# Rows for the experts turned once, the norm's weights applied at the first gathered tile, and a router product in four column groups

## The chip, the cores and the metric

The kernel runs on one core of a Trainium2 chip. The metric is device time in microseconds (us). The engines go by these names: PE multiplies matrices (PEld is its weight load), ACT and DVE evict and split tiles, POOL does small arithmetic and issues indirect transfers, SP issues the loads of the weight stream. Engines run on their own and meet at semaphores.

## What is computed

One inference step of a decoder with two layers, on 288 token rows (256 prompt, 32 sample) of 1024 features. Each layer mixes tokens and then applies a feed-forward part; in the second layer that part is a choice of 2 out of 8 experts:

```python
h = rmsnorm(x, g_ffn[1])
logits = h @ w_router                    # 8 per row
vals, idx = top_k(logits, 2); wts = softmax(vals)
for e in range(8):
    out += gates[:, e] * (silu(h @ wg[e]) * (h @ wu[e])) @ wd[e]
x = x + out
```

where `rmsnorm(x, g)` is `x * rsqrt(mean(x*x) + eps) * g`: one factor for each row (the code's `rstd`) and one for each feature (the norm's weights `g`).

## The kernel before

All weights come from HBM once, as a stream of chunks of 128 x 2048 fp32 (1 MB) into a ring of six buffers `raw`. ACT copies a chunk into a rounded high part `whi` (L311), DVE subtracts for the low part `wlo` (L315), and PE forms each product from three matmuls (L327 to L329). Rings of three `whi` and `wlo` let PE hold ACT back, and ACT DVE.

`xT` holds the rows turned, features on the 128 partitions in eight blocks `k`. The stretch between the last product of layer 1's mixing and the first product of expert 0 is what the change touches. It goes like this, each engine in its own written order:

- ACT makes `xg[k] = xT[k] * g` (`with_gain`, L580; g lies there one to a partition) and squares, POOL adds the squares up in `ssum` (L448).
- PE forms the router product (`route`, L1805): eight matmuls, one for each `k`, into 8 partitions of one bank, then the sums of squares (`sums_of_x`, L1536). DVE copies the logits (L1210) and the means (L949), and POOL makes `rstd` from them (L452).
- PE turns `xg` back into rows, six blocks of four transposes each (`row_block`, L1858), the first of them ahead of the turned logits (L1866).
- DVE takes the logits (L1215), finds the two largest and the mask, signals `pos_in`, clears the third row tile of `xm` (L1230, signal `xm_blank`), and after PE's counts (L1875, L1877) makes the place of each row: `rounds_ok`, the selection matrix `sel` (L1250), `to_row` (L1261). Then it splits a chunk (L315).
- ACT evicts the six blocks into `xm`, times `rstd` (L761). PE turns `xT` itself into rows, six more blocks, which ACT evicts into `x` (L766), to which the experts' results are added.
- PE gathers the rows of expert 0 (`gather`, L1897): `xm` times `sel` gives eight blocks of 128 features x 128 places in two banks. ACT rounds each bank into `gT_hi` (`gathered_hi`, L792), DVE subtracts for `gT_lo` (`gathered_lo`, L1340), and PE begins expert 0 with chunks 66 and 67, then 68.
- POOL scatters the rows of `xm` to HBM, six indirect transfers (L515, signal `x_spread`), from which ACT's queue loads the rows of expert 1 onwards (L833). ACT waits there, in its own order, ahead of all that follows in expert 0.

The rounding copies in expert 0's first steps need a table load on ACT (before L792), as do SiLU and Exp later (L797, L878).

Of the kernel before, what the change touches and what calls it, by code (L numbers as in the profile page):

```python
# [64 lines left out]
FILL_LEFT = NE * SLOTS - FILL * (UP_CH - UP_CH % RAWS)  # L65
SETTLES = 12
NEVER = -3.0e38
NORMS = 7
# [24 lines left out]
def build(nc, io):  # L93
# [3 lines left out]
    with ctx:  # L97
# [19 lines left out]
        def phase():  # L117
            return ExitStack()

        early = phase()  # L120
        ph = lambda n, s, d=F: early.enter_context(nc.sbuf_tensor(n, s, d))
# [50 lines left out]
        with phase() as room:  # L172
# [18 lines left out]
            xm = ph("xm", [P, 3, D])  # L191
            logitsT = ph("logitsT", [NE, NT])
            logits = ph("logits", [P, 3, NE])
# [50 lines left out]
        for width in (W_POOL, W_SP, W_SPS, G_V, S_POOL):  # L244
# [31 lines left out]
            "y_hi_out", "y_out", "y_last_out", "y_half_done", "scat_done", "x_added", "fin_out",  # L276
            "to_row_out", "from_row_out", "got_added", "zero_set", "crossed_in", "sP_out", "hx_packed", "pair_in", "pair_out", "left_hi", "left_lo", "xn_blank", "xg_out", "xm_blank", "xm_turned", "ticked", "settled")}
        zero_filled, x_spread, rows_in, y_saved = (sem(n) for n in ("zero_filled", "x_spread", "rows_in", "y_saved"))
# [14 lines left out]
        GOT_STEPS = {4: (0, 1), 5: (2,), 6: (3, 4), 7: (5,), 8: (6, 7), 9: (8,), 10: (9, 10), 11: (11,)}  # L293
        TURN_BANKS = (0, 1, 6)
        ROW_BANKS = (3, 4, 5, 6, 7, 2)
# [75 lines left out]
        def _(sp):  # L371
# [26 lines left out]
            for c in range(C_MIX1, C_MOE):  # L398
                load_chunk(sp, (c, c), c % RAWS)
            sp.wait_ge(S["dT_done"], 4 * DEPTH)  # L400
            for c in range(C_MOE, C_MOE + RAWS):
                load_chunk(sp, (c, c), c % RAWS)
            sp.wait_ge(S["rounds_ok"], 1)
            n_rounds = nc.sync.value_load(rounds[0:1, 0:1], min_val=1, max_val=MAX_ROUNDS)
            with nc.sync.Fori(0, n_rounds) as r:
                done = nc.sync.snap(1 >> r)
                with nc.sync.Fori(done, ROUND_CH // RAWS) as i:
                    for j in range(RAWS):
                        row = C_MOE + RAWS * i + j
                        load_chunk(sp, (row + ROUND_CH * r, row), (C_MOE + j) % RAWS)  # L410
            sp.dma_start(g_rows, io["g_final"]).then_inc(gain_in, 16)
            for t in range(3):
# [8 lines left out]
        def _(pool):  # L421
# [44 lines left out]
            pool.wait_ge(chunk_used, DEPTH * KV_CH)  # L466
            zero_pair(qs[0:1])
            for l in range(DEPTH):
                if l:
# [31 lines left out]
                if l == 0:  # L501
# [5 lines left out]
                    fill(pool, y_slots[Y_ROWS:Y_ROWS + P, :], P)  # L507

            pool.wait_ge(zero_filled, 16 * FILLS)
            pool.wait_ge(S["xm_out"], 6)  # L510
# [31 lines left out]
        def _(act):  # L542
# [212 lines left out]
            act.wait_ge(rstd_ok, rstd_event(1, E_FFN))  # L755
            for t in range(3):
                if t == 2:
                    act.wait_ge(S["xm_blank"], 1)
                for n in range(2):
                    act.wait_ge(S["xm_turned"], 2 * t + n + 1)  # L760
                    nc.scalar.activation(xm[0:ROWS[t], t, n * 512:(n + 1) * 512], bank[ROW_BANKS[2 * t + n]][0:ROWS[t], :],  # L761
                                         ACT.Copy, scale=rstd[0:ROWS[t], N_FFN, t:t + 1]).then_inc(S["xm_out"], 1)
            for t in range(3):
                for n in range(2):
                    act.wait_ge(S["rows_turned"], 2 * t + n + 1)
                    nc.scalar.activation(x[0:ROWS[t], t, n * 512:(n + 1) * 512], bank[ROW_BANKS[2 * t + n]][0:ROWS[t], :],  # L766
                                         ACT.Copy).then_inc(S["x_rows_out"], 1)

# [3 lines left out]
            with nc.scalar.Fori(0, n_rounds) as r:  # L772
# [17 lines left out]
                def gathered_hi(q, j, b):  # L790
                    act.wait_ge(S["gat_done"], 2 * q + b + 1)
                    nc.scalar.activation(gT_hi[:, j, 4 * b:4 * b + 4, :].rearrange("p a b -> p (a b)"), bank[b][:, :],  # L792
                                         ACT.Copy).then_inc(S["gat_hi"], 1)

                def silu_of(cb, s, extra=0):
# [68 lines left out]
                for b in range(2):  # L864
                    gathered_hi(q, 0, b)
                for slot in range(3):
# [29 lines left out]
        def _(dve):  # L896
# [312 lines left out]
            dve.wait_ge(S["logit_done"], 1)  # L1209
            V.tensor_copy(logitsT[:, :], bank[2][0:NE, 0:NT]).then_inc(S["logitT_out"], 1)  # L1210
            mean_of_x(2, N_FFN, 1)
# [60 lines left out]
            with V.Fori(0, n_rounds) as r:  # L1272
# [65 lines left out]
                def gathered_lo(q, j, b):  # L1338
                    dve.wait_ge(S["gat_hi"], 2 * q + b + 1)
                    V.tensor_tensor(gT_lo[:, j, 4 * b:4 * b + 4, :].rearrange("p a b -> p (a b)"), bank[b][:, :],  # L1340
                                    gT_hi[:, j, 4 * b:4 * b + 4, :].rearrange("p a b -> p (a b)").bitcast(F), ALU.subtract)\
                        .then_inc(S["gat_lo"], 1)

                def keep_selT():
                    dve.wait_ge(S["selT_done"], r + 1)
                    V.tensor_copy(selT[:, :], bank[0][:, 0:NT]).then_inc(S["selT_out"], 1)
# [108 lines left out]
                for b in range(2):  # L1455
                    gathered_lo(q, 0, b)
                with V.Fori(V.snap((1 >> r) * 2), 3) as m:
# [29 lines left out]

            dve.wait_ge(gain_in, 16)
            for t in range(3):
# [7 lines left out]
        def _(pe):  # L1497
# [95 lines left out]
            for l in range(DEPTH):  # L1593
# [208 lines left out]
                def route(k):  # L1802

                    pe.wait_ge(S["xg_out"], k + 1)
# [56 lines left out]
            pe.wait_ge(S["xg_out"], 4)  # L1861
            row_block(0, 0, xg).then_inc(S["xm_turned"], 1)
            pe.wait_ge(S["logitT_out"], 1)
            pe.wait_ge(ms_out, 3)
            for t in range(3):
                last = T.transpose(bank[1][0:ROWS[t], L_AT + t * NE:L_AT + (t + 1) * NE], logitsT[:, t * P:t * P + ROWS[t]],  # L1866
                                   ident[0:NE, 0:NE])
            last.then_inc(S["logit_turned"], 1)
            pe.wait_ge(S["xg_out"], KD)
            for t, n in ((0, 1), (1, 0), (1, 1), (2, 0), (2, 1)):  # L1870
                row_block(t, n, xg).then_inc(S["xm_turned"], 1)

# [6 lines left out]
            last.then_inc(S["pos_done"], 1)  # L1879
            for t in range(3):  # L1880
                for n in range(2):
                    pe.wait_ge(S["xm_out"], 2 * t + n + 1)
                    row_block(t, n, xT).then_inc(S["rows_turned"], 1)
# [308 lines left out]
```

## Time and profile before

| | us |
|---|---|
| median of three runs | 1460.87 (1460.55 to 1461.44) |
| span of the profiled execution | 1460.6 |
| PE busy | 1432.0 (98%) |
| DVE busy | 1178.8 (81%) |
| ACT busy | 958.8 (66%) |
| POOL busy | 113.0 (8%) |
| load of weights, 427.91 MB on SP's queue | 77.0% of 16 engines' span |

The span of the profile, from the first to the last instruction, is 0.2 us below the median of the runs. Busy time of pipelined matmuls overlaps, so how full PE is has to be read from the chain of waits: the work that ended last, followed back step by step to what released it.

### The profile page before, as it was taken

To read this page: it belongs to the slowest core of one execution; us is meant where nothing else is said; L and a number is where in the kernel's file an instruction comes from. 1 tells how busy PE (TensorE), PEld (TensorE's weight loads), DVE (VectorE), ACT (ScalarE), POOL (GpSimd) and SP (SyncE) were. 2 spreads that over 40 slices of the span, in tenths; PEclk is the share of its full clock that TensorE was granted. 3 is DMA by queue.
4 is the path that set the end of the run, shared out by engine and by line. 5 is a ranking of instruction groups with operands and counts; after the bars stand their busy time and mean duration, and the time that the engine had idled before them with its cause. 6 is when DMAs were issued, how large, how long until landed. Compare 5 with 4: busy or idle time off the path is not lost.

```text
span 1460.6 us, 21408 instructions
## 1 busy us (share of the span) xinstructions
PE 1432.0 (98%) x7550; PEld 1218.0 (83%) x7550; DVE 1178.8 (81%) x1125; ACT 958.8 (66%) x929; POOL 113.0 (8%) x125
## 2 busy tenths in 40 slices
PE   7999999999999999999999999999999999999997
PEld 5999999999988788888888888888888887888785
DVE  5767766645675888988988888898898888899997
ACT  7646343344566877777777777777777777777774
POOL 1312111001313000000000000000000000002100
PEclk9999999999999999999999999999999999999999
DMA  9643687655433999999999999999999999999992
GB/s 358 259 151 142 235 277 260 227 190 184 179 117 117 385 367 363 367 381 371 349 398 365 356 396 367 357 376 362 373 349 407 366 356 390 365 361 364 402 397 109
DMA packets 67425, 456.31 MB, mean 312 GB/s; under 512 B 7652, under 2 KB 7946, under 8 KB 15911
## 3 DMA queue, kind: packets, MB, share of 16 engines
q1 hardware_dynamic: 59687, 427.91, 77.0%
q0 software_dynamic: 5680, 20.49, 3.6%
q10 hardware_dynamic: 2016, 7.34, 1.2%
q8 instruction: 27, 0.44, 0.1%
q14 instruction: 15, 0.12, 0.0%
HBM read 434.10 MB, written 21.88 MB: 312 GB/s over the span
## 4 chain that ended last, share of the span: by engine, by line
PE 89%; DVE 4%; ACT 4%; DMA 1%; issue 1%; POOL 0%; DVEq 0%; SPq 0%; ACTq 0%
PE bank L328 28%; PE bank L327 27%; PE bank L329 27%; DVE wlo L315 2%; PE bank L1926 2%; ACT whi L311 1%; DMA raw<-in_stream 1%; ACT junk L553 1%; PE bank L1686 0%; DMA stage<-in_mem 0%; PE bank L1904 0%; PE bank L1555 0%; PE bank L1554 0%; DVE stage L1112 0%; PE bank L1858 0%
## 5 line engine op out<-in xcount | busy, mean ns | idle before, releaser
L315 DVE TENSOR_TENSOR wlo<-raw,whi 128x2048 fp32r<-128x2048 f32 x400 | 916.1, 2293 | 153.6 <-ACT whi L311 152.4
L311 ACT ACTIVATE whi<-raw 128x2048 fp32r<-128x2048 f32 x400 | 765.3, 1915 | 157.0 <-PE bank L329 148.7
L327 PE MATMUL bank<-whi,gT_hi 128*128 128x512 f32 x896 | 362.8, 405 | 0.0
L328 PE MATMUL bank<-wlo,gT_hi 128*128 128x512 f32 x896 | 354.8, 396 | 0.0
L329 PE MATMUL bank<-whi,gT_lo 128*128 128x512 f32 x896 | 354.3, 395 | 0.0
L329 PEld LDWEIGHTS bank<-whi,gT_lo 128*128 128x128 f32 x896 | 168.2, 188 | 39.8
L327 PEld LDWEIGHTS bank<-whi,gT_hi 128*128 128x128 f32 x896 | 168.4, 188 | 36.2
L328 PEld LDWEIGHTS bank<-wlo,gT_hi 128*128 128x128 f32 x896 | 168.7, 188 | 35.7
L328 PE MATMUL bank<-wlo,eT_hi 128*128 128x512 f32 x448 | 177.4, 396 | 0.0
L327 PE MATMUL bank<-whi,eT_hi 128*128 128x512 f32 x448 | 176.5, 394 | 0.9 <-DVE eT_lo L1355 0.9
L329 PE MATMUL bank<-whi,eT_lo 128*128 128x512 f32 x448 | 177.2, 395 | 0.0
L327 PE MATMUL bank<-hT_hi,whi 128*128 128x288 f32 x512 | 153.1, 299 | 1.9 <-DVE hT_lo L917 1.6
L328 PE MATMUL bank<-hT_lo,whi 128*128 128x288 f32 x512 | 152.1, 297 | 0.0
L329 PE MATMUL bank<-hT_hi,wlo 128*128 128x288 f32 x512 | 152.0, 297 | 0.0
L801 ACT ACTIVATE eT_hi<-bank 128x256 fp32r<-128x256 f32 x112 | 43.2, 386 | 118.0 <-PE bank L1926 118.0
L327 PEld LDWEIGHTS bank<-whi,eT_hi 128*128 128x128 f32 x448 | 84.1, 188 | 22.3 <-DVE wlo L315 1.3
L328 PEld LDWEIGHTS bank<-wlo,eT_hi 128*128 128x128 f32 x448 | 84.1, 188 | 20.5
L329 PEld LDWEIGHTS bank<-whi,eT_lo 128*128 128x128 f32 x448 | 84.1, 188 | 19.9
L327 PEld LDWEIGHTS bank<-hT_hi,whi 128*128 128x128 f32 x512 | 96.7, 189 | 2.7 <-DVE hT_lo L917 2.1
L328 PEld LDWEIGHTS bank<-hT_lo,whi 128*128 128x128 f32 x512 | 96.5, 189 | 0.1
L329 PEld LDWEIGHTS bank<-hT_hi,wlo 128*128 128x128 f32 x512 | 96.6, 189 | 0.0
L528 POOL TENSOR_TENSOR tick<-half 128x3 f32<-128x3 f32 x2 | 2.6, 1288 | 863.3 <-DMA y_slots<-y_rows 863.3
(268 smaller groups left out, 1410.5 us busy)
## 6 DMA issues: line engine op xcount, KB each, us to landing
raw<-in_stream SPq DMA_DIRECT2D x401, 1024.0 KB, 5.3
x_slots<-zero POOLq DMA_DIRECT2D x18, 640.0 KB, 5.7
rows_e<-x_slots ACTq DMA_DIRECT2D x7, 512.0 KB, 6.5
y_slots<-y_rows ACTq DMA_DIRECT2D x7, 512.0 KB, 6.3
const<-in_const SPq DMA_DIRECT2D x1, 1192.0 KB, 22.3
raw<-in_stream SPq DMA_DIRECT2D x2, 512.0 KB, 6.9
stage<-in_mem SPq DMA_DIRECT2D x2, 512.0 KB, 7.2
xn<-in_x_prompt SPq DMA_DIRECT2D x1, 1024.0 KB, 10.4
```

The costliest lines, as they stand in the source:

```text
L311: nc.scalar.activation(whi[:, slot % SPL, :], raw[:, slot, :], ACT.Copy).then_inc(hi_ready, 1)
L315: nc.vector.tensor_tensor(wlo[:, slot % SPL, :], raw[:, slot, :], whi[:, slot % SPL, :].bitcast(F), ALU.subtract).then_inc(lo_ready, 1)
L327: nc.tensor.matmul(out, a_hi, b_hi, start=start, stop=False, **kw)
L328: nc.tensor.matmul(out, a_hi, b_lo, start=False, stop=False, **kw)
L329: return nc.tensor.matmul(out, a_lo, b_hi, start=False, stop=stop, **kw)
L528: nc.gpsimd.tensor_tensor(tick[:, :], half[:, :], half[:, :], ALU.mult).then_inc(S["ticked"], 1)
L553: last = nc.scalar.activation(junk[0:r, 0:src.shape[-1]], src[0:r, t, :], ACT.Square, accum_out=ss[0:r, n, t:t + 1])
L801: nc.scalar.activation(eT_hi[:, s % 2, :, :].rearrange("p a b -> p (a b)"), bank[4 + s % 2][:, 0:256], ACT.Copy).then_inc(S["eT_hi_out"], 1)
L1926: last = T.transpose(bank[4 + s % 2][:, b * P:(b + 1) * P], eh[:, s % 2, b * P:(b + 1) * P], ident)
```

## The change

- `xm` is filled from `xT`, times `rstd` only; so its six blocks serve twice, for `xm` and for `x`, and PE's six blocks of `xg` are gone. The blocks come in another order (`BLOCKS`: left halves first), two of them ahead of the turned logits. ACT now waits for `xm_blank` ahead of all six.
- The weights g are applied where the first gathered tile is evicted: ACT's two copies of 128 x 512 become eight of 128 x 128 with a factor for each partition (`first_hi`), DVE's two subtractions eight of the same size (`first_lo`).
- The rows scattered to HBM need g too: SP loads it in rows (`g_moe`, 512 KB) ahead of the first chunks of the experts, and POOL multiplies three tiles of 1024 columns into `got` before it scatters.
- The router's weights lie in blocks of 32 columns (8 used, built by POOL early on), and the eight products go to four groups of 32 columns, two to each. The logits are turned by a matmul with a matrix `gather8`, which adds the four groups up.

```diff
 # ACT
-            for t in range(3):
-                if t == 2:
-                    act.wait_ge(S["xm_blank"], 1)
-                for n in range(2):
-                    act.wait_ge(S["xm_turned"], 2 * t + n + 1)
-                    nc.scalar.activation(xm[...], bank[ROW_BANKS[2 * t + n]][...], ACT.Copy, scale=rstd[...])
-            for t in range(3):
-                for n in range(2):
-                    act.wait_ge(S["rows_turned"], 2 * t + n + 1)
-                    nc.scalar.activation(x[...], bank[ROW_BANKS[2 * t + n]][...], ACT.Copy)
+            act.wait_ge(S["xm_blank"], 1)
+            for i, (t, n) in enumerate(BLOCKS):
+                act.wait_ge(S["rows_turned"], i + 1)
+                nc.scalar.activation(xm[...], bank[ROW_BANKS[2 * t + n]][...], ACT.Copy, scale=rstd[...])
+            for t, n in BLOCKS:
+                nc.scalar.activation(x[...], bank[ROW_BANKS[2 * t + n]][...], ACT.Copy)
...
+                def first_hi(q, b):
+                    act.wait_ge(S["gat_done"], 2 * q + b + 1)
+                    for k in range(4 * b, 4 * b + 4):
+                        last = nc.scalar.activation(gT_hi[:, 0, k, :], bank[b][:, k % 4 * P:(k % 4 + 1) * P], ACT.Copy,
+                                                    scale=gains[:, 1, G_FFN, k:k + 1])
...
 # POOL
+            pool.wait_ge(gain_in, 16)
+            pool.wait_ge(S["xm_out"], 6)
+            for t in range(3):
+                nc.gpsimd.tensor_tensor(got[0:r, t, :], xm[0:r, t, :], g_rows[0:r, :], ALU.mult)
+            pool.wait_ge(S["xm_gained"], 3)
...
-                        in_=xm[0:r, t, :], in_offset=None).then_inc(x_spread, 16)
+                        in_=got[0:r, t, :], in_offset=None).then_inc(x_spread, 16)
...
 # DVE
-            V.tensor_copy(logitsT[:, :], bank[2][0:NE, 0:NT])
+            V.tensor_copy(logitsT[:, :], bank[2][:, 0:NT])
...
+                    for k in range(4 * b, 4 * b + 4):
+                        last = V.scalar_tensor_tensor(out=gT_lo[:, 0, k, :], in0=bank[b][...], scalar=gains[:, 1, G_FFN, k:k + 1],
+                                                      in1=gT_hi[:, 0, k, :], op0=ALU.mult, op1=ALU.subtract)
...
 # PE
-                    m = T.matmul(bank[2][0:NE, 0:NT], router[:, k, :], xg[:, k, :], start=k == 0, stop=k == KD - 1)
+                    quad = slice(k % 4 * QUAD, (k % 4 + 1) * QUAD)
+                    m = T.matmul(bank[2][quad, 0:NT], routers[:, k, :], xg[:, k, :], start=k < 4, stop=k >= 4)
...
-            row_block(0, 0, xg)
+            for t, n in BLOCKS[0:2]:
+                row_block(t, n, xT)
             pe.wait_ge(S["logitT_out"], 1)
             pe.wait_ge(ms_out, 3)
             for t in range(3):
-                last = T.transpose(bank[1][...], logitsT[...], ident[0:NE, 0:NE])
+                last = T.matmul(bank[1][...], logitsT[...], gather8, start=True, stop=True)
-            for t, n in ((0, 1), (1, 0), (1, 1), (2, 0), (2, 1)):
-                row_block(t, n, xg)
+            for t, n in BLOCKS[2:]:
+                row_block(t, n, xT)
...
-            for t in range(3):
-                for n in range(2):
-                    pe.wait_ge(S["xm_out"], 2 * t + n + 1)
-                    row_block(t, n, xT)
...
+                pe.wait_ge(S["xm_out"], 3)
                 gather(0)
+                pe.wait_ge(S["xm_out"], 6)
                 gather(1)
```

## Rows read from the trace of the kernel before

**Rows 1.** The page: span, and the chain that ended last, by engine.

```profile
span 1460.6 us, 21408 instructions
...
PE 89%; DVE 4%; ACT 4%; DMA 1%; issue 1%; POOL 0%; DVEq 0%; SPq 0%; ACTq 0%
```

**Rows 2.** The chain in order of time, 440 to 490: start, us, what.

```profile
455.60 4.04 PE bank L1805 x16
459.64 0.76 PE bank L1536 x6
...
461.13 2.33 PE bank L1858 x20
...
464.26 2.67 PE bank L1858 x24
466.94 5.41 PE bank L1897 x48
472.34 0.23 PE bank L327
...
483.81 1.92 ACT whi L311
```

**Rows 3.** Timeline of ACT: start, us, engine, line, operation, tiles, count [idle before].

```profile
461.68 3.53 ACT L761 ACTIVATE xm<-bank,rstd 128x512 f32<-128x512 f32 x6 [4.77 <-POOL rstd L452]
465.12 2.96 ACT L766 ACTIVATE x_eps<-bank 128x512 f32<-128x512 f32 x6
468.10 1.28 ACT L792 ACT_TABLE_LOAD   x1
...
472.38 0.60 ACT L792 ACTIVATE gT_hi<-bank 128x512 fp32r<-128x512 f32 x1 [2.08 <-PE bank L1897]
...
493.93 0.43 ACTq L833 DMA_DIRECT2D rows_e<-x_slots  x1
...
497.38 1.92 ACT L311 ACTIVATE whi<-raw 128x2048 fp32r<-128x2048 f32 x1 [1.72 <-PE bank L329]
```

**Rows 4.** Timeline of DVE, 446 to 482.

```profile
461.17 0.30 DVE L1215 COPY logits<-bank 128x8 f32<-128x8 f32 x3 [0.57 <-PE bank L1866]
...
462.90 0.91 DVE L1230 MEMSET xm<- 128x1024 f32 x1 [0.15 <-issue]
...
466.91 2.27 DVE L315 TENSOR_TENSOR wlo<-raw,whi 128x2048 fp32r<-128x2048 f32 x1
```

**Rows 5.** Timeline of POOL, at the start and around the experts' rows.

```profile
72.70 0.20 POOL L437 TENSOR_SCALAR ms<-ss 128x3 f32<-128x3 f32 x1 [19.75 <-ACTq L557]
...
457.06 0.79 POOL L448 TENSOR_TENSOR ssum<-ssum,sq 128x288 f32<-128x288 f32 x1 [0.55 <-ACT sq L591]
...
467.78 2.41 POOL L515 DMA_INDIRECT x_slots<-xm,to_row  x1 [6.18 <-DVE to_row L1261]
```

**Rows 6.** Groups by line and shape: busy us, mean ns, idle before.

```profile
L562 ACT ACTIVATE hT_hi<-bank,const 128x288 fp32r<-128x288 f32 x16 | 7.6, 499 | 10.7 <-PE bank L1514 10.7
...
L917 DVE SCALAR_TENSOR_TENSOR hT_lo<-bank,const,hT_hi 128x288 fp32r<-128x288 f32 x16 | 7.9, 510 | 7.5 <-ACT hT_hi L562 7.5
```

**Rows 7.** Indirect transfers, L515 and landing, landing of L531: ns min/median/max, starts.

```profile
L515 POOL DMA_INDIRECT x_slots<-xm,to_row x6: 874/971/2785, 467.8 to 475.5; - x6
...
DMA to landing us min/median/max: 7.0/8.0/9.2
...
DMA to landing us min/median/max: 9.5/11.7/13.0
```

**Rows 8.** The scores, row halves alternating, 362.9 to 365.3, by line.

```profile
L1625 PE MATMUL bank<-kT,qT x16: 376/376/480, 363.2 to 364.8; 64*128 64x256 f32 x16
```

**Rows 9.** Stretches: us, PE PEld DVE ACT POOL busy (count), granted clock, DMA share, GB/s.

```profile
109.64:113.00 3.36, 1.67 (x13) 1.28 (x12) 1.94 (x6) 2.29 (x7) 1.16 (x2) 1.00 0.02 5
113.00:116.40 3.40, 3.40 (x20) 2.95 (x19) 1.87 (x5) 1.87 (x1) 0.00 (x0) 0.50 0.00 0
...
455.46:466.94 11.48, 11.34 (x83) 8.31 (x84) 6.38 (x51) 6.13 (x12) 2.62 (x4) 1.00 0.00 1
```

More of the change, by code:

```diff
@@ L66 @@
 SETTLES = 12
+QUAD = 32
 NEVER = -3.0e38
@@ L118, in phase @@
             return ExitStack()
+        routers = ctx.enter_context(nc.sbuf_tensor("routers", [P, KD, QUAD], F))
+        gather8 = ctx.enter_context(nc.sbuf_tensor("gather8", [P, NE], F))[:, :]
         early = phase()
@@ L191, in build @@
             xm = ph("xm", [P, 3, D])
-            logitsT = ph("logitsT", [NE, NT])
+            logitsT = ph("logitsT", [P, NT])
             logits = ph("logits", [P, 3, NE])
@@ L276, in build @@
             "y_hi_out", "y_out", "y_last_out", "y_half_done", "scat_done", "x_added", "fin_out",
-            "to_row_out", "from_row_out", "got_added", "zero_set", "crossed_in", "sP_out", "hx_packed", "pair_in", "pair_out", "left_hi", "left_lo", "xn_blank", "xg_out", "xm_blank", "xm_turned", "ticked", "settled")}
+            "to_row_out", "from_row_out", "got_added", "zero_set", "crossed_in", "sP_out", "hx_packed", "pair_in", "pair_out", "left_hi", "left_lo", "xn_blank", "xg_out", "xm_blank", "xm_turned", "ticked", "settled", "xm_gained", "routers_out")}
         zero_filled, x_spread, rows_in, y_saved = (sem(n) for n in ("zero_filled", "x_spread", "rows_in", "y_saved"))
@@ L294, in build @@
         TURN_BANKS = (0, 1, 6)
+        BLOCKS = ((0, 0), (1, 0), (2, 0), (0, 1), (1, 1), (2, 1))
         ROW_BANKS = (3, 4, 5, 6, 7, 2)
@@ L400, in _ @@
             sp.wait_ge(S["dT_done"], 4 * DEPTH)
+            sp.dma_start(g_rows, io["g_moe"]).then_inc(gain_in, 16)
             for c in range(C_MOE, C_MOE + RAWS):
@@ L410, in _ @@
                         load_chunk(sp, (row + ROUND_CH * r, row), (C_MOE + j) % RAWS)
+            sp.wait_ge(S["xm_gained"], 3)
             sp.dma_start(g_rows, io["g_final"]).then_inc(gain_in, 16)
@@ L467, in _ @@
             zero_pair(qs[0:1])
+            pool.wait_ge(const_in, 16)
+            link(nc.gpsimd.memset(routers[:, :, :], 0.0))
+            nc.gpsimd.tensor_copy(routers[:, :, 0:NE], router).then_inc(S["routers_out"], 1)
+            for q in range(P // QUAD):
+                at = slice(q * QUAD, (q + 1) * QUAD)
+                pool.wait_ge(S["routers_out"], 1 + q)
+                nc.gpsimd.tensor_copy(gather8[at, :], ident[at, q * QUAD:q * QUAD + NE]).then_inc(S["routers_out"], 1)
+            pool.wait_ge(S["routers_out"], 1 + P // QUAD)
             for l in range(DEPTH):
@@ L507, in _ @@
                     fill(pool, y_slots[Y_ROWS:Y_ROWS + P, :], P)
+            pool.wait_ge(gain_in, 16)
+            pool.wait_ge(S["xm_out"], 6)
+            for t in range(3):
+                r = ROWS[t]
+                nc.gpsimd.tensor_tensor(got[0:r, t, :], xm[0:r, t, :], g_rows[0:r, :], ALU.mult).then_inc(S["xm_gained"], 1)
+            pool.wait_ge(S["xm_gained"], 3)
             pool.wait_ge(zero_filled, 16 * FILLS)
-            pool.wait_ge(S["xm_out"], 6)
             pool.wait_ge(S["to_row_out"], 1)
@@ L755, in _ @@
             act.wait_ge(rstd_ok, rstd_event(1, E_FFN))
-            for t in range(3):
-                if t == 2:
-                    act.wait_ge(S["xm_blank"], 1)
-                for n in range(2):
-                    act.wait_ge(S["xm_turned"], 2 * t + n + 1)
-                    nc.scalar.activation(xm[0:ROWS[t], t, n * 512:(n + 1) * 512], bank[ROW_BANKS[2 * t + n]][0:ROWS[t], :],
-                                         ACT.Copy, scale=rstd[0:ROWS[t], N_FFN, t:t + 1]).then_inc(S["xm_out"], 1)
-            for t in range(3):
-                for n in range(2):
-                    act.wait_ge(S["rows_turned"], 2 * t + n + 1)
-                    nc.scalar.activation(x[0:ROWS[t], t, n * 512:(n + 1) * 512], bank[ROW_BANKS[2 * t + n]][0:ROWS[t], :],
-                                         ACT.Copy).then_inc(S["x_rows_out"], 1)
+            act.wait_ge(S["xm_blank"], 1)
+            for i, (t, n) in enumerate(BLOCKS):
+                act.wait_ge(S["rows_turned"], i + 1)
+                nc.scalar.activation(xm[0:ROWS[t], t, n * 512:(n + 1) * 512], bank[ROW_BANKS[2 * t + n]][0:ROWS[t], :],
+                                     ACT.Copy, scale=rstd[0:ROWS[t], N_FFN, t:t + 1]).then_inc(S["xm_out"], 1)
+            for t, n in BLOCKS:
+                nc.scalar.activation(x[0:ROWS[t], t, n * 512:(n + 1) * 512], bank[ROW_BANKS[2 * t + n]][0:ROWS[t], :],
+                                     ACT.Copy).then_inc(S["x_rows_out"], 1)
             act.wait_ge(S["rounds_ok"], 1)
@@ L793, in gathered_hi @@
                                          ACT.Copy).then_inc(S["gat_hi"], 1)
+                def first_hi(q, b):
[3 more added lines that the diff above has]
+                                                    scale=gains[:, 1, G_FFN, k:k + 1])
+                    last.then_inc(S["gat_hi"], 1)
                 def silu_of(cb, s, extra=0):
@@ L864, in _ @@
                 for b in range(2):
-                    gathered_hi(q, 0, b)
+                    first_hi(q, b)
                 for slot in range(3):
@@ L1209, in _ @@
             dve.wait_ge(S["logit_done"], 1)
-            V.tensor_copy(logitsT[:, :], bank[2][0:NE, 0:NT]).then_inc(S["logitT_out"], 1)
+            V.tensor_copy(logitsT[:, :], bank[2][:, 0:NT]).then_inc(S["logitT_out"], 1)
             mean_of_x(2, N_FFN, 1)
@@ L1342, in gathered_lo, with first_lo @@
                         .then_inc(S["gat_lo"], 1)
+                def first_lo(q, b):
+                    dve.wait_ge(S["gat_hi"], 2 * q + b + 1)
+                    for k in range(4 * b, 4 * b + 4):
+                        last = V.scalar_tensor_tensor(out=gT_lo[:, 0, k, :], in0=bank[b][:, k % 4 * P:(k % 4 + 1) * P],
+                                                      scalar=gains[:, 1, G_FFN, k:k + 1], in1=gT_hi[:, 0, k, :].bitcast(F),
+                                                      op0=ALU.mult, op1=ALU.subtract)
+                    last.then_inc(S["gat_lo"], 1)
                 def keep_selT():
@@ L1455, in _ @@
                 for b in range(2):
-                    gathered_lo(q, 0, b)
+                    first_lo(q, b)
                 with V.Fori(V.snap((1 >> r) * 2), 3) as m:
@@ L1486, in _ @@
                     expert(NE - 2 + j, j, j == 1)
-            dve.wait_ge(gain_in, 16)
+            dve.wait_ge(gain_in, 32)
             for t in range(3):
@@ L1860, in row_block @@
                 return last
-            pe.wait_ge(S["xg_out"], 4)
-            row_block(0, 0, xg).then_inc(S["xm_turned"], 1)
+            pe.wait_ge(S["xg_out"], KD)
+            for t, n in BLOCKS[0:2]:
+                row_block(t, n, xT).then_inc(S["rows_turned"], 1)
             pe.wait_ge(S["logitT_out"], 1)
@@ L1865, in _ @@
             for t in range(3):
-                last = T.transpose(bank[1][0:ROWS[t], L_AT + t * NE:L_AT + (t + 1) * NE], logitsT[:, t * P:t * P + ROWS[t]],
-                                   ident[0:NE, 0:NE])
+                last = T.matmul(bank[1][0:ROWS[t], L_AT + t * NE:L_AT + (t + 1) * NE], logitsT[:, t * P:t * P + ROWS[t]],
+                                gather8, start=True, stop=True)
             last.then_inc(S["logit_turned"], 1)
-            pe.wait_ge(S["xg_out"], KD)
-            for t, n in ((0, 1), (1, 0), (1, 1), (2, 0), (2, 1)):
-                row_block(t, n, xg).then_inc(S["xm_turned"], 1)
+            for t, n in BLOCKS[2:]:
+                row_block(t, n, xT).then_inc(S["rows_turned"], 1)
             pe.wait_ge(S["pos_in"], 1)
```

3 lines of the change are left out of this document (2 added, 1 removed).

## The prediction, made before the changed kernel was run

> **What bounds the kernel now.** I read the chain of waits first: the reader should see that PE holds 89% of it [rows 1]. In order of time the chain stays on PE, without a gap, from the router at 455.60 to expert 0's first product at 472.34 [rows 2]: every microsecond taken from PE there could reach the end, if nothing else is late. So I read the other engines' timelines over the same stretch, for how much later than PE each would be. ACT ends its twelve evictions of rows at 468.08, has its table at 469.38, and waits for PE only 2.08 us ahead of its last gathered copy [rows 3]. It is the next bound, close behind. DVE and POOL have more room, and from 483.81 the chain goes over ACT and its table loads until PE is full again [rows 2]; that piece starts when PE has done with chunk 69, so a shift of PE's start goes through it whole.
>
> **The change part by part.** All times are this execution's. Its span is 1460.6, the median of the runs 1460.87; what I add to the one I add to the other.
>
> Router. Before: 16 records (two passes a product) in 4.04 us, 0.25 each [rows 2]. After: a product's second pass can run beside the next product's first, in another column group. No row shows column groups side by side. The nearest has two row halves alternating: 16 records of 256 columns start within 1.6 us, 0.107 each, where 0.25 x 256/288 = 0.22 would be one after the other [rows 8]; so two at a time. Taken: 8 x 0.25 + 0.25 = 2.25, ending at 457.85. Ends: 1.0 (four at a time) and 4.04 (none). Below 2.25 nothing is won anyway: the sums of squares wait for POOL's last addition, done at 457.06 + 0.79 = 457.85 [rows 5]. They start at 458.0, not at 459.64: 1.65 earlier. The logits' copy on DVE moves with them.
>
> Turned logits. Before them stand now two blocks, 8 transposes of 2.33/20 = 0.117 [rows 2], and they are six records of an fp32 product, at the price of the six sums, 0.76 [rows 2]. 458.0 + 0.76 + 0.93 + 0.76 = 460.45, against 461.13 [rows 2], so DVE's logits begin at 460.5 and not at 461.17 [rows 4]. Of 1.65 us some 0.7 is left.
>
> The wait moved ahead. ACT's first eviction now waits for `xm_blank`. DVE signals that when its clearing ends, at 462.90 + 0.91 = 463.81, which is 2.64 after its logits began [rows 4]: after, 463.15. So ACT starts at 463.2, where it had started at 461.68 when `rstd` came [rows 3]. The blocks from PE lie ready by then (four more, 16 x 0.117, end at 462.35). Behind that wait, on ACT, is everything that PE needs: six evictions to `xm`, six to `x`, the table load, together 469.38 - 461.68 = 7.70 [rows 3]. ACT has its table at 470.9, 1.5 later than before.
>
> Gather. PE saves 24 transposes, 2.67 us, ahead of it [rows 2]; the counts end near 463.15 and not 464.26, so the gather starts at about 465.8 and ends, 5.41 later, at 471.2 instead of 472.34 [rows 2]. It needs three, then six evictions to `xm`: there at 465.0 and 466.8. This saving is hidden: PE then waits for ACT.
>
> First eviction. ACT: 288 columns with a factor take 499 ns [rows 6], 2048 take 1.92 [rows 3], so 0.8 ns a column and 0.37 us for 128; one follows another by about 0.1 less (six `xm` evictions of like form take 0.59 each [rows 3]). Four: 3 x 0.27 + 0.37 = 1.2, against 0.60 [rows 3]. Ends: 0.9 and 2.0 (four at the full 499). DVE, the same way: 510 ns for 288 [rows 6], 2.27 for 2048 [rows 4], so 0.35 for 128, four in 1.1 (0.9 to 2.0). ACT 470.9 + 1.2, DVE + 1.1, two handoffs of 0.05 to 0.1: PE's first product of expert 0 starts at 473.4, where it had started at 472.34: **+1.1**. The second bank's copies run on behind and are done before chunk 67 is multiplied.
>
> Behind that. ACT splits chunk 68 from 473.35, DVE from 475.4 to 477.7; PE wants it two chunks (24 products at 0.23 [rows 2]) after 473.4, at 479.0: 1.3 of slack. The piece over ACT from 483.81 starts 1.1 later, too, and gives nothing back.
>
> POOL's products. 0.79 us for 288 columns; with 0.20 for a short operation as the fixed part [rows 5], 1024 columns take 2.3 us (0.79 if length were free, 2.81 in full proportion). Three: 6.9, from ACT's sixth eviction at 466.8 or, if POOL is held, from the end of DVE's split (466.91 + 2.27 [rows 4], now about 1.1 earlier). They end at 473.7 to 475, and the six scatters, which began at 467.78 [rows 5], begin there. They go between DVE's splits, some 2.2 each (the record of 2.41 against a median of 0.97 shows one held [rows 5, 7]); the last starts at 485 to 488 and lands 7.0 to 9.2 later [rows 7], at 492 to 497. ACT waits for them at 493.93 + 1.1 = 495.0 [rows 3], and can be 1.7 late at no cost, since a little further on it waits 1.72 for PE [rows 3]. Taken at nothing; the end of the range is among the rivals.
>
> At nothing: the load of `g_moe`, half a chunk's bytes ahead of the experts' first chunks on SP's queue (covered by the projections ahead of the router, in which the experts' first chunks come in; uncovered, half a chunk's landing); the six small operations on POOL in layer 0 (POOL stands idle for 19.75 us right behind its stores [rows 5]); the semaphores.
>
> Sum: 1460.87 + 1.1 = **1462.0**.
>
> The Trainium skill (SBUF — State Buffer, "Who interferes with whom") has a rule against this change: a DVE instruction with two SBUF inputs and a GpSimd instruction that reads SBUF hold each other off for a whole instruction, whichever starts first. The trace shows the one half of it, POOL held by DVE's split (2.41 for 0.97); no row shows a split held by POOL. By that rule the third product, if it still runs at 475.4, holds chunk 68.
>
> **The rivals.**
>
> A. PE's clock falls in its new waits (2.6 us ahead of the gather, 2.2 behind it). In layer 0 PE was busy 1.67 of 3.36 us, and the granted clock, 1.00 until then, was 0.50 for the next 3.40, that is 1.2 GHz for 2.4 [rows 9]. If that falls on expert 0's first products, half of 3.40 is lost: +1.7 more, 1463.7. Against it: the small products up to 466.94 left the clock at 1.00 [rows 9].
>
> B. The column groups don't overlap. Router 4.04, sums at 459.64 as before; all steps from there as above come 1.65 later, +2.75: 1463.6. If the wider weight load showed as well, by 0.05 a record, 1464.4.
>
> C. The slower side: the scatters land late. Place: ACT's wait ahead of expert 1's rows. With products of 2.81, and landings of up to 13.0, as indirect transfers later in the kernel have under the full stream [rows 7], they are there by 488 + 13 = 501, 6 after ACT. It decides from 496.7 on, where ACT's 1.7 are used up: up to +4.3 more, 1466.3. For it: they now run beside the full stream. Against it: this scatter landed in 9.2 at most, beside the stream too.
>
> D. POOL's products hold DVE's split of chunk 68 for up to a product of 2.81; less 1.3 of slack, +1.5: 1463.5.
>
> E. PE's saving reaches the end: ACT is not late, because its evictions start at `rstd` and the wait for `xm_blank` ends early. Then the gather's end is the bound, 471.2 for 472.34, and the two evictions cost 0 to 1: 1459.7 to 1460.9. The order written out on DVE speaks against it.
>
> **How the numbers follow.** Forecast 0.50, A 0.20, B 0.07, C 0.11, D 0.05, E 0.07. A measurement of this kernel can tell about 0.2% from no change, which is 2.9 us: 1457.95 to 1463.79. The forecast, D and E lie within; of A and B about two in five pass 1463.79 with the forecast's own half microsecond of error, of C about half, and combinations add some: slower 0.22. Faster would need PE to start expert 0 before 469.4, where even the gather has not ended: 0.04. Same 0.74. The range reaches below to E's gain, 1459.6, and above to A or C with an error on top, 1464.6.
>
> **What would show it.** Right: in the trace after, ACT's first L761 waits for DVE's clearing, at about 463.2; PE idles about 2 us between the gather's end and the first gate product; that product starts near 473.4. The router's records take about 2.3 us and the sums start right behind POOL's last addition. Wrong: ACT evicting before the clearing, no gap behind the gather, router records 0.25 apart, clock below 1.00 near 471 to 477, or ACT waiting ahead of its load of `rows_e`.

## The result, and the profile after

| | before | after |
|---|---|---|
| median of four runs each, us | 1461.05 (1460.55 to 1461.44) | 1446.63 (1445.02 to 1448.02) |
| profiled execution, its span | 1460.6 | 1446.2 |
| PE busy | 1432.0 | 1410.3 |
| chain of waits, PE's share | 89% | 89% |

After to before 0.9905, 95% interval 0.9893 to 0.9917: 14 us faster, where +1.1 was forecast. The chain of waits of the changed kernel in the touched stretch (start, us, what, as in [rows 2]):

```profile
455.54 0.80 POOL ssum L454
456.38 0.83 PE bank L1568 x6
...
458.68 0.31 DVE logits L1238 x3
...
460.41 0.92 DVE xm L1253
461.49 1.27 ACT xm L778 x2
...
467.90 1.28 ACT L814
470.10 0.26 ACT gT_hi L814
470.64 0.87 DVE gT_lo L1371 x3
471.63 0.50 PE bank L331
```

The chain no longer stays on PE. It goes over POOL's last addition, DVE's clearing of `xm`, ACT's twelve evictions and table, to the first gate product. The timelines of PE, ACT and POOL there (columns as in [rows 3]):

```profile
454.23 1.55 PE L1840 MATMUL bank<-stage,routers 128*32 128x288 f32 x16 [0.30 <-PE bank L333]
463.81 5.62 PE L1928 MATMUL bank<-sel,xm 128*128 128x128 f32 x48 [2.44 <-DVEq L1292]
471.63 0.50 PE L331 MATMUL bank<-whi,gT_hi 128*128 128x512 f32 x1 [2.19 <-DVE gT_lo L1371]
...
461.49 3.53 ACT L778 ACTIVATE xm<-bank,rstd 128x512 f32<-128x512 f32 x6 [6.09 <-DVE xm L1253]
...
465.16 7.98 POOL L527 TENSOR_TENSOR got<-xm,const 128x1024 f32<-128x1024 f32 x3 [6.76 <-ACT xm L778]
```

Before, the router starts at 455.60 [rows 2] and the first gate product at 472.10 (its record just ahead of the chain's 472.34):

```profile
472.10 0.47 PE L327 MATMUL bank<-whi,gT_hi 128*128 128x512 f32 x1
```

So from router to experts it is 16.50 before and 471.63 - 454.23 = 17.40 after. The router starts 0.44 after the start of the mixing's last matmul before (455.16) and 0.59 after it now (453.64): in all the change is 1.05 **later** there, as forecast. The gain isn't in the touched stretch. It is in what the change left alone: from the first product of expert 0 to the last of expert 7, 976.02 us before (472.10 to 1448.12) and 962.02 after (471.63 to 1433.65), for the same 4032 products. The windows of a full stretch of that stage, first before, then after (columns as in [rows 9]):

```profile
500.00:600.00 100.00, 100.00 (x447) 80.61 (x446) 87.81 (x60) 73.66 (x60) 0.00 (x0) 1.00 0.96 368
1000.00:1100.00 100.00, 100.00 (x447) 80.55 (x446) 88.91 (x61) 73.45 (x62) 0.00 (x0) 1.00 0.97 362
```

```profile
500.00:600.00 100.00, 100.00 (x455) 81.95 (x454) 89.08 (x60) 74.69 (x62) 0.00 (x0) 1.00 0.98 371
1000.00:1100.00 100.00, 100.00 (x454) 81.95 (x453) 90.37 (x63) 75.17 (x63) 0.00 (x0) 1.00 0.96 373
```

PE is busy throughout in both, at full clock; yet it gets 7 or 8 matmuls more into each 100 us. The mean distance from one start to the next, worked out from the start times of the 512-column products between 500 and 1340, is 233.3 ns before and 228.9 after (229.0 with gT loaded, 228.7 with eT), and this from the stage's beginning to its end. 4032 x 4.4 ns = 17.7 us. Counted in a run without a fall of the clock in that stage (e1, below), 15.5 arrive; here it is 14.0, for the clock fell at the start of it:

```profile
472.50:476.00 3.50, 3.50 (x10) 2.76 (x9) 2.33 (x2) 0.68 (x1) 3.20 (x2) 0.51 0.00 0
```

This is rival A: 1.2 GHz on expert 0's first products, behind PE's two idles of 2.44 and 2.19. The two profiles differ by 14.4: these 14.0, and 0.5 by which expert 0 starts earlier, since the mixing ended 1.5 earlier in this execution.

### The profile page after: what moved, and what is told of

Its sections match the earlier page's. It is cut to its first block, busy times and chain, and to the rows that moved or that the text cites. A ratio compares the mean times of both kernels' runs of the same rounds, so it can differ in the third digit from the quotient of the medians.

```text
span 1446.2 us, 21391 instructions
## 1 busy us (share of the span) xinstructions
PE 1410.3 (98%) x7529; PEld 1213.7 (84%) x7529; DVE 1179.2 (82%) x1131; ACT 959.5 (66%) x935; POOL 122.2 (8%) x134
## 4 chain that ended last, share of the span: by engine, by line
PE 89%; DVE 4%; ACT 4%; DMA 1%; issue 1%; POOL 0%; DVEq 0%; ACTq 0%; SPq 0%; POOLq 0%
PE bank L333 28%; PE bank L332 27%; PE bank L331 27%; DVE wlo L319 2%; PE bank L1957 2%; ACT whi L315 1%; DMA raw<-in_stream 1%; ACT junk L572 1%; PE bank L1718 0%; DMA stage<-in_mem 0%; PE bank L1935 0%; PE bank L1587 0%; PE bank L1586 0%; DVE stage L1135 0%; PE bank L1546 0%
```

## The experiments

Two theories for the faster products. **I**: the instructions, the code's place or the new operations. **S**: the place in SBUF. The change declares two tensors, `routers` (1024 bytes a partition) and `gather8` (32 bytes), ahead of `xT`; so all phase tensors behind them, gT and eT among them, lie 1056 bytes higher, while raw, `whi`, `wlo` and `const` stay. In the experts gT and eT are what PE loads as weights (the row's `128*128`), `whi` and `wlo` what streams through. I call **distance** the start of gT_hi less the start of `whi`, worked out from the sizes of the tensors declared between, each rounded up to 32 bytes, modulo 512 (all blocks and slots of these tensors are multiples of 512 bytes apart): 416 before, 448 after. The traces hold no addresses. If the rounding is another, all the distances below shift by one and the same number, and their differences stand.

### Place or instructions

```diff
 # e1_pad32; e2_pad1024 has 256 for 8; e3_after_pad32 adds the line to the changed kernel
+        ctx.enter_context(nc.sbuf_tensor("pad", [P, 8], F))
         early = phase()
 # e4_experts_pad32, this alone
+            ph("pad", [P, 8])
             gT_hi = ph("gT_hi", [P, 2, KD, P], FR)
```

> The kernel before with one unused tensor of 32 bytes a partition set ahead of `xT`; no instruction differs, every tensor of the phases lies 32 bytes higher, while raw, whi, wlo and const stay. Theory S (the place in SBUF: in the kernel before, gT_hi and the other phase tensors begin 32 bytes past a multiple of 64, in the changed kernel on one, and PE's matmuls run faster there): the experts' 512-column products are spaced 229 ns and not 233, 4030 of them give 17 us, and the mixing some 1.5 more: 1442.5 to 1445. Theory I (the instructions: PE's loop stands at another place of the code, or the column groups and the saved transposes change what PE does later): nothing changes here, 233 ns, 1460 to 1462.

> The same with 1024 bytes in place of 32: the phase tensors are moved by about as much as in the changed kernel, but stay 32 past a multiple of 64. Theory S in its form with 64 bytes: 233 ns, 1460 to 1462. Theory S in another form (the distance between gT and whi, or a larger block of the memory, decides): 229 ns, 1442 to 1446. Theory I: 1460 to 1462.

> The changed kernel with 32 bytes more ahead of `xT`: every instruction of the change is there, and the phase tensors lie again 32 past a multiple of 64. Theory S: the gain is gone, 233 ns, and what is left is the change by itself as forecast, 1.05 later at the experts' start and some 1.7 if the clock falls there: 1461.5 to 1464. Theory I: 229 ns and 1445 to 1448, as the changed kernel.

> The kernel before with 32 bytes ahead of gT_hi, in the experts' phase alone: attention, mixing and the dense part keep their places, the experts' tensors (gT, eT, rows, xm) move. Theory S: the experts' 17 us come, the mixing's 1.5 don't: 1443 to 1445.5, and the mixing ends at 455.5 as before. Theory I: 1460 to 1462.

Measured, against 1460.94 for the kernel before: e1 1444.62 (ratio 0.9891, 0.9871 to 0.9911), e2 1460.82 (0.9998, 0.9989 to 1.0007), e3 1463.01 (1.0015, 1.0004 to 1.0025), e4 1445.32 (0.9891, 0.9873 to 0.9909). The same window of e1 and of e3:

```profile
500.00:600.00 100.00, 100.00 (x454) 81.95 (x453) 89.74 (x62) 75.00 (x61) 0.00 (x0) 1.00 0.98 366
```

```profile
500.00:600.00 100.00, 100.00 (x447) 80.47 (x446) 87.77 (x60) 73.11 (x60) 0.00 (x0) 1.00 0.96 363
```

Theory I falls. Thirty-two bytes that nobody reads give the kernel before the whole gain, and 32 bytes more take it from the changed kernel. For this gain the experts' tensors are enough (e4). In e1 the stage takes 960.51 us, 15.5 less than before. Its distances from one start to the next of up to 0.3 us add up to 17.3 less (932.9 to 915.6), the longer ones, in which PE waits or does other work, to 1.8 more (43.1 to 44.9). And e1 is 2.0 us below the changed kernel at the same distance. That would be the change by itself, but the runs overlap (1443.96 to 1447.72 and 1445.02 to 1448.02). e3, spaced 233.3 like the kernel before, is 2.1 us above that kernel, and the whole of its interval lies above 1; but by the profiles some 0.8 of this is the dense part, where 527 recorded products with `HT` streaming are 133.3 ns apart for 131.8. The mixing's 1.5 us, which I had put down to the place, can't be told from the spread of the profiled executions: in e4, where the mixing's tensors lie as before, the router starts at 453.16, 2.4 earlier than before.

### Which side, and which distance

```diff
 # e5_whi_off
+        sb("pad", [P, 8])
         whi = sb("whi", [P, SPL, CW], FR)
 # e6_gT_only: e4's line, and
+            ph("pad2", [P, 8])
             rows_e = ph("rows_e", [P, D])
 # e9_both_off: e5's line and e1's
 # e8_pad480, e12_pad160, e13_pad96, e14_pad352, e15_pad544: e1's line with 120, 40, 24, 88, 136 for 8
```

> The kernel before with 32 bytes set ahead of whi: now whi, wlo and const begin 32 past a multiple of 64, and the phase tensors (gT, eT, HT, xT), 32 higher too, on one. In the experts gT and eT are what PE loads as weights, whi and wlo what it streams through. Theory W (the loaded side alone counts): 229 ns, 1443 to 1447. Theory M (the streamed side counts as much): both gains and losses, 233 ns or more, 1460 and above. In the dense part the sides are the other way round, so by W its 288-column products (132 to 133 ns) get slower, by at most some 4 ns.

> 32 bytes ahead of gT_hi and 32 more behind gT_lo: gT alone begins on a multiple of 64, eT stays 32 past one. If the place of each loaded tile decides for its own matmuls: gate and up (two thirds of the products) at 229 ns, down at 233, so two thirds of 16 us: 1449 to 1451. If it is the start of the whole phase, or only eT: 1444 to 1446 or 1460.

> The kernel before with 480 bytes ahead of xT, so that the phase tensors begin on a multiple of 1024 (with 32 bytes they begin on 64, not on 128). If 64 is all that counts: as with 32 bytes, 1443.5 to 1446. If larger blocks count as well: below 228 ns and 1443.

> The kernel before with 32 bytes ahead of whi and 32 more ahead of xT: whi and wlo begin 32 past a multiple of 128, gT and eT 96 past one, so both sides are off 64, but stand 64 apart as in the changed kernel. Theory D (the distance of the loaded side from the streamed side, within 128 bytes, counts: 64 is free, 32, 0 and 96 are not): 229 ns, 1443 to 1447. Theory A (each side has to begin on a multiple of 64 by itself): 233 ns or more, 1459 to 1462.

> The kernel before with 160 bytes ahead of xT: 128 more than the 32 that gave the gain, so that the loaded side stands again 64 past a multiple of 128 from the streamed side, but at the other place within 256 and 512. If the distance counts within 128 bytes: 229 ns and 1443.5 to 1446. If it counts within a larger block: above 232 ns, 1457 to 1461.

> The kernel before with 96 bytes ahead of xT: distance 512, a multiple of 512, so each loaded block of 512 bytes stands level with the streamed one. If level blocks collide most: 233 ns or more, 1459 to 1463. If only odd multiples of 32 cost in full, as 896 suggests: 232.4 ns, 1456 to 1458.5. If it is free as 448 is: 229 ns, 1443.5 to 1446.

> The same with 352 bytes: distance 768, half a block of 512 from level. If the two streams are furthest apart there and distance as such helps: 229 ns, 1443.5 to 1446. If 448 is a place of its own: 232 to 233.5 ns, 1456 to 1462.

> The same with 544 bytes: distance 960, 448 within 512. If the distance counts within 512 bytes, in which all blocks of gT, eT, whi and wlo repeat: 229 ns, 1443.5 to 1446. If within 1024 or more: 232 ns or above, 1456 to 1462.

Sorted by distance; ns are the mean from start to start with gT and with eT loaded, behind each time is that of the kernel before beside it on the same chip:

| distance | run | gT, ns | eT, ns | us (before) |
|---|---|---|---|---|
| 0 | e13 | 228.0 | 226.8 | 1440.90 (1460.18) |
| 64 | e12 | 233.4 | 233.4 | 1461.50 (1459.70) |
| 256 | e14 | 228.1 | 226.8 | 1442.67 (1460.18) |
| 384 | e8 | 232.4 | 232.9 | 1457.20 (1459.87) |
| 416 | before, e2, e5 | 233.3 | 233.3 | e5 1460.23 (1459.87) |
| 448 | after, e1, e4, e9, e15 | 228.9 to 229.0 | 228.7 | e9 1445.46 (1461.67), e15 1444.04 (1460.18) |
| 480 | e3; eT in e6 | 233.3 | 233.3, 233.4 | e6 1450.59 (1459.87) |

Windows of e13, e12 and e6, in this order:

```profile
500.00:600.00 100.00, 100.00 (x457) 82.44 (x457) 89.89 (x62) 75.33 (x62) 0.00 (x0) 1.00 0.98 369
```

```profile
500.00:600.00 100.00, 100.00 (x446) 80.59 (x445) 88.17 (x59) 73.68 (x61) 0.00 (x0) 1.00 0.95 364
```

```profile
500.00:600.00 100.00, 100.00 (x451) 81.39 (x450) 89.01 (x61) 74.40 (x62) 0.00 (x0) 1.00 0.97 369
```

And of e5 and e9:

```profile
500.00:600.00 100.00, 100.00 (x446) 80.54 (x445) 88.06 (x59) 73.48 (x62) 0.00 (x0) 1.00 0.96 366
```

```profile
500.00:600.00 100.00, 100.00 (x454) 81.97 (x453) 89.63 (x61) 75.23 (x62) 0.00 (x0) 1.00 0.99 368
```

e6 has gT at 448 and eT at 480: 229.2 and 233.4 ns, and 1450.6, 9.3 us of the 15.6 to 16.3 that come with both at 448; gT's products are two thirds of all. So each product answers for its own loaded tile. e5 and e9 show that it is the distance and not either side's own start: in e5 gT stands where e1 has it, and only `whi`, `wlo` and the tensors declared between them and `xT` lie elsewhere than in e1, and the gain is gone; in e9 both are moved, the distance is 448 again, and it is back. `raw` kept its place, so gT stands as far from it in e5 as in e1: that distance isn't it either. e8, which I had expected as fast as e1 or faster, was slow (232.4 and 232.9). My next guess, that 64 counts within 128 bytes, fell with e12 (576, 64 within 512, slow). e15 (960) shows that 448 repeats after 512 bytes, e13 and e14 that 0 and 256 are alike and the best. All seven distances would also agree with a rule within 256 bytes; no run took a pair apart there. Whether it is the load or the stream that waits, and for what, no row shows: a load's mean is 188 ns in both kernels.

### The change by itself: where its earlier start went

```diff
 # e7_early_clear, on the changed kernel (DVE)
             V.memset(x_eps[:, :, D:D + 1], (EPS * D) ** 0.5)
+            V.memset(xm[:, 2, :], 0.0).then_inc(S["xm_blank"], 1)
             dve.wait_ge(S["logit_done"], 1)
...
-            V.memset(xm[:, 2, :], 0.0).then_inc(S["xm_blank"], 1)
 # e10_clear_products_later: e7, and on POOL
             pool.wait_ge(gain_in, 16)
+            pool.wait_ge(lo_ready, C_MOE + 2)
             pool.wait_ge(S["xm_out"], 6)
 # e11_products_on_dve: e7, with POOL's products taken out, and on DVE
+            def gain(t):
+                V.tensor_tensor(got[0:ROWS[t], t, :], xm[0:ROWS[t], t, :], g_rows[0:ROWS[t], :], ALU.mult).then_inc(S["xm_gained"], 1)
             lo_static(dve, C_MOE + 1)
+            gain(0)
...
                     first_lo(q, b)
+                    gain(1 + b)
```

> The changed kernel, its layout kept, with DVE's clearing of the third row tile of xm moved ahead of the wait for the router. By the prediction's steps ACT's wait for that clearing is what delays it: ACT then starts at rstd, near 458.5 and not 461.5, has its table by 466.3, and PE goes from the gather into expert 0 without the 2.19 of idle: 2.2 earlier, and up to 3.9 if the clock then doesn't fall: 1442.5 to 1444.5. If the wait is not what holds ACT (blocks from PE, or POOL's products, are), 1446 to 1447.

> The changed kernel with the clearing moved ahead, as in the run before, and POOL's three products waiting until DVE has split chunk 67. There sel took 4.98 us and rounds 2.34 because POOL's products ran beside them (0.66 and 0.15 in the changed kernel). Theory H (POOL's products held DVE): sel at 0.7 again, the gather starts some 9.2 after the router's start and PE goes from it into expert 0 without idling, some 14.7 after the router's start (17.4 in the changed kernel, 16.5 in the kernel before): 1442 to 1445, the lower end if the clock doesn't fall at the experts' start. If something else held DVE there: 1450 to 1453 again.

> The run before started expert 0 as early as forecast (14.93 after the router, no fall of the clock) and lost it again: POOL's products and then its scatters, held by DVE's splits, ended at 488.2, and ACT got the rows of expert 1 only at 497.88, with 5.06 of waiting behind it. Here the clearing stays ahead and the three products go to DVE, into its own gaps (one behind the split of chunk 67, one behind each half of the first gathered tile), 1.13 each by half a split; POOL scatters a tile as soon as its product is there. If the late scatters are what the run before lost: the six scatters end by 480, ACT's load of rows_e waits for nothing, expert 0 starts 14.9 to 15.6 after the router: 1442.5 to 1444.5, below both the kernel before with 32 bytes ahead (1444.6) and the changed kernel. If something else took it: 1446 to 1447.5 again.

e7 took 1452.19, 5.6 **more** than the changed kernel, where 2.2 to 3.9 less was expected. Its timelines of PE, DVE and POOL:

```profile
468.25 7.54 PE L1928 MATMUL bank<-sel,xm 128*128 128x128 f32 x48 [8.96 <-DVEq L1292]
...
460.08 2.34 DVE L1268 TENSOR_TENSOR rounds<-over 1x1 int32<-1x1 f32 x1
462.35 4.98 DVE L1273 TENSOR_SCALAR sel<-const,posm 128x128 f32<-128x128 f32 x3
...
460.07 6.99 POOL L527 TENSOR_TENSOR got<-xm,const 128x1024 f32<-128x1024 f32 x3 [3.75 <-ACT xm L778]
```

ACT was free as expected, but POOL's products now began 10 ns ahead of DVE's `rounds`, which took 2.34 us for 0.15, and the selection 4.98 for 0.66. In the changed kernel they are:

```profile
462.16 0.15 DVE L1268 TENSOR_TENSOR rounds<-over 1x1 int32<-1x1 f32 x1
462.24 0.66 DVE L1273 TENSOR_SCALAR sel<-const,posm 128x128 f32<-128x128 f32 x3
```

`rounds` waits out the first product, the three operations of `sel` the other two, at 2.33 each. It is the mechanism of rival D, on operations that I hadn't thought of. In the changed kernel the hoisted wait for `xm_blank` held the products back (to 465.16) until DVE was past the selection.

e10 took 1447.06, above the 1442 to 1445 that were expected. With POOL's products later, `sel` is back at 0.66, so they were what held it. The gather runs straight into expert 0: 469.44 - 454.51 = 14.93 for 17.40, the clock at 1.00 throughout. The 2.5 us are lost again 30 us later (DVE, POOL, the chain, ACT):

```profile
462.44 0.66 DVE L1274 TENSOR_SCALAR sel<-const,posm 128x128 f32<-128x128 f32 x3
...
472.81 3.04 DVE L1493 TENSOR_TENSOR wlo<-raw,whi  x1 [0.82 <-ACT whi L895]
...
487.31 0.86 POOL L535 DMA_INDIRECT x_slots<-got,to_row  x1 [0.30 <-issue]
...
487.31 10.24 DMA x_slots<-got,to_row
...
497.88 0.41 ACTq L857 DMA_DIRECT2D rows_e<-x_slots  x1
498.57 0.39 ACT L821 ACTIVATE esg<-bank 128x256 f32<-128x256 f32 x1 [5.06 <-PE bank L333]
```

That is rival C: the products ended at 473.7; the scatters ran beside DVE's splits, where five of them took 1.74 to 2.91 us, and the last, beside none, 0.86; the last landed 10.24 us after its start at 487.31 by the chain. ACT waited there ahead of what PE needs to go on; the row puts its 5.06 down to a product of PE, the chain to the transfer. Rival D shows as well: the split of chunk 68 at 472.81 takes 3.04 for 2.29 in the changed kernel, beside the last product.

e11 took 1445.16, just above the 1442.5 to 1444.5 expected. ACT's load of `rows_e` starts at 491.90, and its next eviction shows no idle, so the late scatters were the loss. But expert 0 starts 469.83 - 453.10 = 16.73 after the router and not 14.9: the clock fell during the gather, behind 2.55 of idle (PE, the window, then ACT).

```profile
462.79 7.25 PE L1929 MATMUL bank<-sel,xm 128*128 128x128 f32 x48 [2.55 <-DVEq L1292]
...
462.70:466.30 3.60, 3.51 (x18) 3.51 (x19) 3.59 (x6) 2.34 (x4) 0.00 (x0) 0.56 0.74 223
...
491.90 0.42 ACTq L851 DMA_DIRECT2D rows_e<-x_slots  x1
493.27 0.38 ACT L815 ACTIVATE esg<-bank 128x256 f32<-128x256 f32 x1
```

48 products took 7.25 for the 5.62 of the changed kernel. The idle of some 2.5 ahead of the gather is in e10 as well, where the clock stayed. Why it falls in one and not in the other is open.

### Both at the best distance

```diff
 # e16_experts_pad96: the kernel before, e4's line with 24 for 8
 # e17_both_best: e11, and e18_after_level: the changed kernel, both with that line and
+        ctx.enter_context(nc.sbuf_tensor("pad2", [P, 120], F))
         early = phase()
```

> The kernel before with 96 bytes in the experts' phase alone, ahead of gT_hi: distance 512 for the experts, the dense part as it was (its 288-column products took 132.1 to 132.9 ns so, 133.8 with 96 bytes ahead of everything). By the place alone: 226.8 to 228 ns in the experts, and up to 1.7 x 1300 = 2.2 us less than with 96 bytes everywhere: 1438.5 to 1441.

> The changed kernel with clearing ahead and the products on DVE, with the distances of the run before this one in both parts (416 before the experts, 512 in them). If its earlier start of expert 0 counts: 1 us below the run before this one; if the clock then falls at the gather, as in the profile of its sister: the same or up to 1 above.

> The changed kernel as it is, with those same distances. By the prediction's steps it is 1.05 later at the start of expert 0 and loses up to 1.7 to the clock there: 1 to 2.8 above the first of these runs, 2.0 if as measured at the other distance. If the change itself had gained something, it would be below it.

Measured against 1459.89: e16 1439.38 (0.9853, 0.9837 to 0.9870), e17 1439.48 (0.9860, 0.9843 to 0.9877), e18 1441.21 (0.9865, 0.9849 to 0.9882). The spacings are the same in all three (228.0 and 226.8), so e18 over e16 is the change by itself: +1.8 by the medians, but the runs overlap here too (1437.88 to 1441.32 and 1438.55 to 1441.97); at distance 448 it was +2.0. From the router to the first gate product e18 takes 471.27 - 453.88 = 17.39, e16 470.41 - 453.92 = 16.49. In e18's profile the clock fell during the gather (7.25 us), which costs nothing there, since the gather isn't what the first product waits for. e16 beats both kernels with no change of its work at all; the reordering of e17 adds nothing to it that these runs show.

## Why the prediction was wrong, point by point

**What failed** is not a term that was sized wrong but one that I left out. The part "At nothing" lists the loads, POOL's six small operations and the semaphores, but not the two new tensors that move all tensors behind them, and the sum takes all that lies behind expert 0's start, with its 0.23 us a product [rows 2], as if it were the same in both kernels. The runs show in its place 233.3 ns at distance 416 and 228.9 at 448: 14.0 us less in the experts' stage, 15.5 where the clock held. Nothing in the trace of before says that it isn't its best: PE is busy without a gap. So "faster would need PE to start expert 0 before 469.4" was false: it started at 471.63, and the time fell by 14. A change of 4.4 ns in each of 4032 products outweighs every difference that I worked out.

**The Trainium skill** (SBUF — State Buffer, "Who interferes with whom") gives PE two separate read ports, one for the moving operand and one for the weight load, and says that PE never waits on anyone; its subject there is contention between engines. If PE's own two reads are as independent as that, no distance between them could matter. The runs show 226.8 to 233.4 ns with nothing but the distance changed; here the measurement decides.

**The touched stretch** went nearly as told, each time counted from the router's start. That its 1.05 comes so close to 1.1 is in part luck, as the point on the first product shows:

- Router: 2.25 forecast, 1.55 measured. The groups overlap more than two at a time, and as forecast this wins nothing beyond POOL's last addition: the sums wait 0.59 for it and start 2.15 after the router (2.4 forecast).
- Turned logits 0.67 (0.76 forecast); DVE has them 4.45 after the router (4.9).
- ACT is held by DVE's clearing: 461.49 with `<-DVE xm L1253`, 7.26 after the router (7.6). Evictions and table 7.69 (7.70). This was the step that decides, and the chain shows it.
- First eviction: four of ACT in 1.14 (1.2), four of DVE in 1.13 (1.1), in the runs that show them apart.
- PE's saved transposes stay hidden: 2.44 of idle ahead of the gather, 2.19 behind it (2.6 and 2.2 forecast).
- First product 17.40 after the router (17.8). The forecast took 472.34, the start of the chain's piece, as the start before; the product's record starts at 472.10. From the router the change is therefore +0.90, not the forecast's 1.1, and the router itself starts 0.15 later behind the mixing, which I had not forecast: together +1.05.
- POOL's products: 2.3 each forecast, 2.33 undisturbed in e7; the 7.98 of the changed kernel holds 1.1 in which the first waited for DVE's split. The scatters begin at 473.44 and ACT waits for nothing at `rows_e`: nothing, as taken.

**The rivals.** A came about in the profile of the changed kernel, at about 1.5 (962.02 against e1's 960.51), and in e3's, while in e18's the clock fell in the gather; it deserved more than 0.20. B fell (1.55). C and D were right as mechanisms and not reached, because the wait for `xm_blank` happened to keep POOL away from DVE's selection and the scatters still within the slack; e7 and e10 show both when the order is changed. E fell as the change stands. By the medians of the two pairs of equal distance the change by itself costs 1.8 to 2.0 us, between the forecast's 1.1 and A's 2.8; as the runs of each pair overlap, what is shown of it is the 1.05 of the traces, and the 1.5 where the clock fell.

For the rule on DVE with two SBUF inputs and POOL, cited in the prediction, the trace now agrees in both directions: POOL's first product waited for a split in the changed kernel, and in e7 DVE's `rounds`, which reads two values from SBUF, waited for a product. `sel`, which reads a tile and one value for each partition, was held too.

## What to carry to other kernels

Before pricing an edit that declares a tensor, list which tensors it moves, and treat the spacing of matmuls in every stage that uses a moved tensor as unknown; a copy of the kernel before with nothing but an unused tensor of that size tells it apart from the edit. Where a stage of such fp32r products has PE busy throughout, vary the distance between the loaded and the streamed operand in steps of 32 bytes before anything else is tuned: here it is worth 20 us of 1460, and it changes the verdict on any other edit that moves memory. A wait that looks like pure loss can be what keeps two engines apart, so look at what starts earlier when it goes.

## What the runs showed of the hardware that I had not expected

- The spacing of fp32r matmuls of 512 columns, with a weight load of 128 x 128 each, depends on the distance of the loaded tile from the streamed tile in SBUF: 226.8 to 228.1 ns at 0 and 256 bytes modulo 512, 229 at 448, 232.4 to 232.9 at 384, 233.3 to 233.4 at 64, 416 and 480. In the dense part `whi` is loaded and 288 columns stream. Where these are of `HT`, which by the sizes starts a multiple of 512 bytes from gT and was moved with it in the runs named here, the spacing follows the place as well, but in another order: 131.8 to 131.9 ns at 416 (before, e2, e5), 132.2 at 0, 256, 384 and 448 (e13, e14, e8, e1), 133.3 at 64 and 480 (e12, e3). Where they are of `hT` it moved between 132.3 and 133.6 and followed no rule that I could find.
- A GpSimd product of 128 x 1024 with two inputs from SBUF takes 2.33 us, and a DVE operation of one element waits it out (2.34 us for 0.15).
- Sixteen fp32 records of the router in four column groups take 1.55 us, in one group 4.04.
- With like idles of PE ahead of the gather (2.4 to 2.6 us), the granted clock fell to half for some 3.5 us in the gather in e11, e17 and e18, behind it in the changed kernel and e3, and not at all in e10.
